# Moving a hybrid encoder block's constants and first transfers ahead of their stages, and a new order of groups in its recurrence

## The chip, the cores and the metric

One core of a Trainium2 chip runs the whole kernel in one launch. The metric is device time in microseconds (us). The engines are TensorE (PE; its weight loads are shown as PEld), VectorE (DVE), ScalarE (ACT), GpSimd (POOL) and SyncE (SP), which issues most of the transfers. A row with a q behind the engine's name (SPq, POOLq) is its sequencer or its DMA queue.

## The reference

The kernel computes one layer of a streaming encoder for 2048 tokens of 1024 features, all in float32. Cut to what matters:

```
u   = rms_norm(x, ln1_g) @ w_in                       # attention and recurrence read columns of u
o_a = diff_attn_mixer(u[:, :1536], ...)               # 4 heads; lam from exp(sum(lq1*lk1)), exp(sum(lq2*lk2))
o_b = rwkv7_mixer(u[:, 1536:], ...)                   # 8 heads of 64:
      # per token: sa = -S kk;  S = S*w + sa b^T + v k^T;  y = S r
h   = x + concat(o_a, o_b) @ w_out
out = h + hier_moe(rms_norm(h, ln2_g), ...)           # 32 experts, 2 of one group of 8 for each token
```

## The kernel before

Five stages follow each other, each a block that all engines enter together once they have ended the one before: `project`, `attend`, `recur`, `merge`, `experts`.

- `project` makes the combined projection by groups of 256 tokens. It keeps the first head's rotated queries and keys in SBUF (`keep["first_head"]`) and writes the rest to scratch in DRAM, among it `chunks`, the recurrence's operands for 32 chunks of 64 tokens, 642 KB each.
- `attend` loads `lams`, `mask` and `ident` (lines 689 to 690), and TensorE and VectorE wait for all three (697, 772). VectorE then works out lambda (775 to 783; ScalarE's exponential for it is line 739) before its first row of maxima (789).
- `recur` runs the recurrence by chunks. Eight heads lie in four pairs, and every small product is 64 wide. Its order is written out by hand. In turn k TensorE works on four chunks at once, named by how far ahead they are: S (chunk k), B (k + 1), A (k + 2), N (k + 3), so 32 chunks take 35 turns. `PE_TURN`, `ACT_TURN` and `DVE_TURN` (823 to 826) give each engine's order in a turn as (group, how far ahead). The engines count their finished groups in one semaphore each, and `on_pe`, `on_act`, `on_dve` turn a group and chunk into the count to wait for. A group is 4 to 16 products into one of four PSUM couples of banks (`ps`), which rotate by one place each turn. TensorE's products have one shared line (937), ScalarE's copies too (1112), and most of VectorE's adds (1147), so they are told apart by their operands.

The groups that matter here, with what their rows show as out<-moving operand,stationary operand:

| Group | What it is | In the rows |
|---|---|---|
| gl, gbk (N) | products inside a chunk; VectorE masks them into `gl` and `g` | rw_ps<-rw_cin |
| bk, v (A) | transposes of b and k, and of v; ScalarE copies them to `rw_tbk` and `rw_sv` | rw_ps<-rw_eye,rw_cin and rw_ps<-rw_ident,rw_cin |
| r1, r2, r3q, r3l, r4 (A), r5 to r8 (B) | steps of inverting a 64x64 triangular matrix, each read back by ScalarE or VectorE before the next | r2 and r3l: rw_w; r3q: rw_q,rw_w; r4: rw_q,rw_l; r6 and r8: rw_ty |
| s0 (B), s1, s2, s3 (S) | solve for sa and add to the state | s1: rw_state,rw_cin; s0: rw_sv,keep_first_head |
| y1, y2 (S) | the output | rw_cin,rw_state and keep_first_head,rw_sv |

r3l is copied by ScalarE to `l8` (`rw_l` in the rows), r4 reads that. s0 of chunk B ends a turn, and s1 adds to its result at the start of the next, waiting first until s0 is complete. The group gl of a turn waits for VectorE's r8 of the turn before. The operands of five chunks are held (`LOADS`); SP loads the next when y1 and the state's update of an old one are done, and `Early.ahead` (1234) issues the merge stage's constants and `w_out` behind the first five.

- `merge` joins both mixers, adds x and routes the tokens, and `experts` runs 64-token blocks of the experts in order. Before its first block VectorE clears `acc` (two buffers), `xf` and `xb`, then makes `te`, from which come the row numbers (`rows`). GpSimd waits for the clearing, writes two columns of zeros to a spare place (1884, it sets the count that the scatters wait for), then gathers the first two blocks' rows (1887).

Of the kernel before, what the change touches and what calls it, by code (L numbers as in the profile page):

```python
# [24 lines left out]
P = 128  # L25
# [10 lines left out]
NPAIR = 4  # L36
# [102 lines left out]
def project(nc, io, dr, first_head):  # L139
    with ExitStack() as ctx:  # L140
        m = Pool(nc, ctx, "pj")
        w_in = m.sb("w_in", [P, KC, N_IN])
# [3 lines left out]
        ident = m.sb("ident", [P, P])  # L146
        ones2 = m.sb("ones2", [P, P])
        cols = m.sb("cols", [P, PC_N])
# [37 lines left out]
        s_aux = m.sem("aux")  # L186
        s_w = [m.sem(f"w{n}") for n in range(4)]
# [51 lines left out]
        def _(sp):  # L239
# [13 lines left out]
            for n in range(2, 4):  # L253
                weights(n)
            for t in range(XT):
                sp.wait_ge(s_tp, t + 1)
                sp.dma_start(xt[:, t, :], io["x"][GT + t * P:GT + (t + 1) * P, :]).then_inc(s_x[t], 16)
# [30 lines left out]
            for t in range(XT):  # L288
                sp.wait_ge(s_x[t], 16 * NG + 32)

# [335 lines left out]
def attend(nc, io, dr, keep):  # L626
    with ExitStack() as ctx:
# [4 lines left out]
        ident = m.sb("ident", [P, P])  # L632
        mask = m.sb("mask", [P, 2, P])
        lams = m.sb("lams", [P, 4, 64])
# [16 lines left out]
        s_const = m.sem("const")  # L651
# [26 lines left out]
        def _(sp):  # L678
# [10 lines left out]
            for dst, src in ((lams[:, :, :], io["lams"]), (mask[:, :, :], io["c_mask"]), (ident[:, :], io["c_ident"])):  # L689
                sp.dma_start(dst, src).then_inc(s_const, 16)  # L690
            load(0)
            for h in range(1, H_A):
                load(h)

        @block.tensor
        def _(pe):
            pe.wait_ge(s_const, 48)
# [73 lines left out]
        def _(dve):  # L771
            dve.wait_ge(s_const, 48)

# [64 lines left out]
def recur(nc, io, dr, keep, ahead):  # L838
    with ExitStack() as ctx:
        m = Pool(nc, ctx, "rw")  # L840
        cin = [m.sb(f"cin{n}", [P, NPAIR, ROW]) for n in range(LOADS)]
        eye = m.sb("eye", [P, C])
        mgbk = m.sb("mgbk", [P, 2, 2 * C])
        mgl = m.sb("mgl", [P, 3, C])
        ident = m.sb("ident", [P, P])
# [3 lines left out]
        tbk = [m.sb(f"tbk{n}", [P, 2, NPAIR, C]) for n in range(RINGS["tbk"])]  # L849
# [13 lines left out]
        s_const = m.sem("const")  # L863
# [12 lines left out]

        def live(c):

            return 0 <= c < NCH
# [8 lines left out]

        def keys(couple):

            return couple.rearrange("p (r a) n -> p r (a n)", r=2)[:, :, 0:NPAIR * C]

        def values(couple, rows):

            return couple[rows, 1::2, 0:2 * C]
# [13 lines left out]
        def _(sp):  # L909
            for dst, src in ((eye[:, :], io["c_eye"]), (mgbk[:, :, :], io["c_mgbk"]), (mgl[:, :, :], io["c_mgl"]),  # L910
                             (ident[:, :], io["c_ident"])):
                sp.dma_start(dst, src).then_inc(s_const, 16)
            for c in range(LOADS):
                sp.dma_start(cin[c][:, :, :], dr["chunks"][c]).then_inc(s_ld[c], 16)
            ahead(sp)
            for c in range(LOADS, NCH):
                sp.wait_ge(s_pe, on_pe["y1", c - LOADS])
                sp.wait_ge(s_dve, on_dve["st", c - LOADS])
                sp.dma_start(cin[c % LOADS][:, :, :], dr["chunks"][c]).then_inc(s_ld[c % LOADS], 16)
# [12 lines left out]
        def _(pe):  # L932
            A, R, V = slice(0, C), slice(C, 2 * C), slice(4 * C, 5 * C)
# [23 lines left out]

            def turn(k):
                S_, B_, A_, N_ = k, k + 1, k + 2, k + 3
                ba, bb, bc, bd = banks(k)  # L960
                xs, xa, xn = cin[S_ % LOADS], cin[A_ % LOADS], cin[N_ % LOADS]
                ga, gn, gs = (g[c % RINGS["g"]] for c in (A_, N_, S_))
                if live(S_):
# [6 lines left out]
                if live(N_):  # L970
                    pe.wait_ge(s_ld[N_ % LOADS], 16 * (N_ // LOADS) + 16)
                    if live(k):
                        pe.wait_ge(s_dve, on_dve["r8", k])
                    for p, r, f, t, u, j in by_features():
                        ins = product(bb[t, j, LO], xn[f, p, A], xn[f, p, b_of(p)])
                    ins.then_inc(s_pe, 1)
                if live(B_):
                    pe.wait_ge(s_dve, on_dve["r4", B_])
                    if live(k - 1):
                        pe.wait_ge(s_act, on_act["y", k - 1])  # L980
                    elif live(k + 1):
                        pe.wait_ge(s_act, on_act["v", k + 1])
                    l = gl[B_ % RINGS["gl"]]
                    for p, r, f, t, u, j in by_features():
                        product(bc[f, p, LO], q2[t, j, :], eye[t, :])
                        ins = product(bc[f, p, HI], l[t, j, 1, :], q2[t, j, :])
                    ins.then_inc(s_pe, 1)
# [1188 lines left out]
```

## Time and profile before

| What | us |
|---|---|
| median of 3 runs | 2983.03 |
| lowest and highest | 2982.71, 2984.04 |
| the profiled execution | 2979.28 |
| its span, first to last instruction | 2977.3 |
| TensorE busy in the span | 2824.1 |
| VectorE, ScalarE, GpSimd busy | 1541.1, 979.8, 644.8 |

Mean granted TensorE clock of the span: 0.981 of full. Rows are those of the profiled execution. Times in a row are the start from the span's begin, then the duration; in square brackets stands how long the engine had been idle and what ended that.

### The profile page before, as it was taken

The page shows a single profiled execution, that of the slowest core. Times are in us where ns is not written, and L with a number is a line of the kernel's source. Part 1 is how long each engine was busy: PE and PEld are TensorE (multiplying, and loading weights), DVE is VectorE, ACT ScalarE, POOL GpSimd, SP SyncE. Part 2 cuts the span into 40 slices and gives each one's busy share as a digit, 9 for nine tenths or more (in the row PEclk, how much of TensorE's full clock was granted, in tenths as well). Part 3 has the DMA queues.
Part 4 walks back from the last instruction along what each step waited for, and adds up shares of the span by engine and source line. Part 5 has one row for each costly group of instructions (what it writes and reads, how often), then busy time and mean ns, then how long its engine had stood idle before and what let it go on. Part 6 is the DMA issues. An engine that isn't in the chain of part 4 may idle for free. (4 is left out here: it accounts for less than half of the span.)

```text
span 2977.3 us, 61430 instructions
## 1 busy us (share of the span) xinstructions
PE 2824.1 (95%) x23130; PEld 1777.5 (60%) x23131; DVE 1541.1 (52%) x3560; ACT 979.8 (33%) x2303; POOL 644.8 (22%) x812
## 2 busy tenths in 40 slices
PE   8999999999979999989999799994999999999999
PEld 6787878778756666679998555452333333333333
DVE  4677676777768988834444577763111111111111
ACT  3343344334437777734444333331000000000000
POOL 0000000000015555611111001002333333333333
PEclk9999999999989999999999999996999999999999
DMA  7111121121130110041111132253889788787663
GB/s 253 61 64 60 48 79 56 50 72 60 52 116 1 44 44 1 1 169 60 62 57 57 45 113 91 94 183 94 286 301 339 249 299 314 276 292 246 251 218 124
DMA packets 187586, 393.03 MB, mean 132 GB/s; under 512 B 15866, under 2 KB 74106, under 8 KB 186576
## 3 DMA queue, kind: packets, MB, share of 16 engines
q1 hardware_dynamic: 166848, 339.34, 33.0%
q0 software_dynamic: 20512, 50.54, 4.9%
q8 instruction: 159, 2.61, 0.4%
q14 instruction: 67, 0.55, 0.1%
HBM read 325.22 MB, written 78.22 MB: 136 GB/s over the span
## 5 line engine op out<-in xcount | busy, mean ns | idle before, releaser
L328 PE MATMUL pj_big<-pj_xnT,pj_w_in 128*128 128x256 f32 x2816 | 634.6, 381 | 2.1 <-DVE pj_xnT L467 1.5
L328 PEld LDWEIGHTS pj_big<-pj_xnT,pj_w_in 128*128 128x128 f32 x2816 | 537.0, 191 | 83.2 <-issue 5.7
L1921 PE MATMUL ex_pgu<-keep_res,ex_xT 128*64 128x512 f32 x2560 | 568.5, 597 | 0.0
L1921 PEld LDWEIGHTS ex_pgu<-keep_res,ex_xT 128*64 128x64 f32 x2560 | 177.1, 137 | 334.5 <-issue 334.5
L2029 DVE TENSOR_TENSOR ex_hh<-ex_sg,ex_pgu 128x256 f32<-128x256 f32 x80 | 33.7, 421 | 583.5 <-ACT ex_sg L1994 583.5
L1939 PE MATMUL ex_py<-keep_res,ex_hT 128*64 128x512 f32 x1280 | 288.3, 592 | 1.0 <-DVE ex_yb L2037 1.0
L767 POOL TENSOR_SCALAR at_tt<-at_e,at_cf 128x512 f32<-128x512 f32 (+3 forms) x160 | 219.7, 1376 | 176.7 <-DVE at_pd L811 164.1
L1440 PE MATMUL mg_po<-keep_res,mg_mix 128*128 128x512 f32 x512 | 232.5, 611 | 6.9 <-DVE mg_mix L1743 6.9
L298 POOL TENSOR_TENSOR pj_m<-pj_qn,pj_cosin 128x256 f32<-128x256 f32 x64 | 46.6, 729 | 823.4 <-DVE pj_qn L528 597.0
L1994 ACT ACTIVATE ex_sg<-ex_pgu 128x256 f32<-128x256 f32 x80 | 30.7, 384 | 581.4 <-PE ex_pgu L1921 581.4
L746 ACT ACTIVATE at_e<-at_sc,at_nmx 128x512 f32<-128x512 f32 (+3 forms) x320 | 197.0, 623 | 61.6 <-DVE at_nmx L789 59.3
L1939 PEld LDWEIGHTS ex_py<-keep_res,ex_hT 128*64 128x64 f32 x1280 | 91.9, 137 | 183.3 <-issue 182.1
L789 DVE TENSOR_REDUCE at_nmx<-at_sc 128x2 f32<-128x1024 f32 (+3 forms) x160 | 169.5, 1060 | 26.5 <-PE at_sc L708 17.8
L1440 PEld LDWEIGHTS mg_po<-keep_res,mg_mix 128*128 128x128 f32 x512 | 98.3, 196 | 124.1 <-issue 116.3
L1851 POOL DMA_INDIRECT ex_xb<-hn_s,ex_idx x80 | 82.5, 1031 | 361.4 <-PE ex_px L1914 351.0
L2037 DVE SCALAR_TENSOR_TENSOR ex_yb<-ex_py,ex_gates,ex_acc 128x512 f32<-128x512 f32 x80 | 60.1, 751 | 181.1 <-PE ex_py L1939 181.1
L732 PE MATMUL at_op<-at_vh,at_pt 128*128 128x128 f32 x1088 | 148.2, 276 | 0.8 <-ACT at_pt L758 0.8
L732 PEld LDWEIGHTS at_op<-at_vh,at_pt 128*128 128x128 f32 x1088 | 135.1, 193 | 1.4 <-ACT at_pt L758 1.0
L526 DVE RECIPROCAL pj_qrr<-pj_qrr 128x256 f32<-128x256 f32 x64 | 111.9, 1749 | 21.6 <-ACT pj_qrr L441 21.6
L1998 ACT ACTIVATE ex_hT<-ex_phT 128x256 f32<-128x256 f32 x80 | 30.7, 384 | 270.2 <-PE ex_phT L1929 270.2
L927 POOL TENSOR_TENSOR rw_w<-keep_first_head,rw_eye 64x256 f32<-64x256 f32 x64 | 46.1, 720 | 337.7 <-DVE keep_first_head L1158 335.8
L328 PE MATMUL pj_big<-pj_w_in,pj_xnT 128*128 128x512 f32 x256 | 112.5, 592 | 0.0
(288 smaller groups left out, 4370.7 us busy)
## 6 DMA issues: line engine op xcount, KB each, us to landing
keep_res<-in_w_exp_gate SPq DMA_DIRECT2D x32, 2048.0 KB, 8.9
keep_res<-in_w_exp_up SPq DMA_DIRECT2D x32, 2048.0 KB, 16.0
keep_res<-in_w_exp_down SPq DMA_DIRECT2D x32, 2048.0 KB, 8.7
chunks_s<-pj_st SPq DMA_DIRECT2D x32, 642.0 KB, 3.9
rw_cin<-chunks_s SPq DMA_DIRECT2D x32, 642.0 KB, 4.1
pj_xt<-in_x SPq DMA_DIRECT2D x20, 512.0 KB, 3.8
mg_xin<-in_x SPq DMA_DIRECT2D x8, 1024.0 KB, 7.3
out<-mg_hb SPq DMA_DIRECT2D x16, 512.0 KB, 3.4
```

The source lines that it names most:

```text
L298: pool.tensor_tensor(m1[:, p % 2, :], qn[:, p % 2, :], cosin[:, 0, :], ALU.mult).then_inc(s_m1, 1)
L328: ins = pe.matmul(out, lhs, rhs, start=(k == 0), stop=(k == KC - 1))
L526: link(dve, ch, dve.reciprocal(qrr[:, p % 2, :], qrr[:, p % 2, :]))
L732: ins = pe.matmul(op[t % 2][:, 0:P], pt[:, u % 2, b * P:(b + 1) * P], vh[h % 2][:, n, :], start=(n == 0), stop=(n == i))
L746: ins = act.activation(e[:, u % RE, c, 0:w], sc[u % 2][:, c, 0:w], ACT.Exp, bias=nmx[:, t % RE, c, s:s + 1], accum_out=sums[:, t % RE, c, ...
L767: pool.tensor_scalar(tt[:, u % 2, 0:w], e[:, u % RE, 1, 0:w], cf[:, t % RE, 1, s:s + 1], None, ALU.mult).then_inc(s_t, 1)
L789: dve.tensor_reduce(nmx[:, t % RE, :, s], sc[u % 2][:, :, 0:w], AX, ALU.max, negate=True)\
L1440: ins = pe.matmul(po[:, n, :], mix[:, x, k, tok], w_out[:, k, 512 * n:512 * n + 512], start=(k == 0), stop=(k == KC - 1))
L1851: pool.indirect_dma_start(xb[:, :], None, hn2, bass.IndirectOffsetOnAxis(idx[:, 0:1], 0), bounds_check=LAST, oob_is_err=False).then_inc(s_ ...
L1921: ins = pe.matmul(pgu[j * BT:(j + 1) * BT, :, :], lhs, wgu[x][:, k, :, j * HE:(j + 1) * HE], start=(k == 0), stop=(k == KC - 1))
L1939: ins = pe.matmul(py[n * BT:(n + 1) * BT, :], hT[:, part, j * BT:(j + 1) * BT], wd[x][:, 2 * j + part, n * HD:(n + 1) * HD], start=(part = ...
L2037: dve.scalar_tensor_tensor(yb[x][:, :], py[:, :], gates[:, bass.ds(b, 1)], acc[x][:, :], ALU.mult, ALU.add).then_inc(s_yb, 1)
```

## The change

Five things change:

1. `ident` and `cols` are loaded once, in `project`, and kept. `mask` and `lams` are loaded in `project` behind its weights (`lams` in the space of `tb`, which is used later). `attend` waits for no constant.
2. The recurrence's constants and chunk 0 (in the space of `w_out`) are loaded in `attend`, behind the second head's loads. `recur` loads chunks 1 to 5 first, and `w_out` once chunk 0 is used up.
3. In a turn of the recurrence bk and v become one group, bkv: twelve products of 128 rows against the 128x128 identity. ScalarE copies it in three copies that count as one group.
4. The order within a turn is new on three engines. s0 belongs to the same turn as s1.
5. In `experts` GpSimd clears `xf` and `xb` itself, gathers the first two blocks before it writes the spare place (now one row of 64 numbers, taken from `rec`), and VectorE clears `acc` after the row numbers.

```diff
-PE_TURN = (("s1", 0), ("gl", 3), ("r5", 1), ("gbk", 3), ("bk", 2), ("r1", 2), ("s2", 0), ("r2", 2), ("s3", 0), ("v", 2), ("r6", 1),
-           ("r3q", 2), ("r3l", 2), ("r7", 1), ("y1", 0), ("r4", 2), ("y2", 0), ("r8", 1), ("s0", 1))
-ACT_TURN = (("s1", 0), ("r5", 1), ("bk", 2), ("r1", 2), ("sa", 0), ("r2", 2), ("v", 2), ("r3l", 2), ("r7", 1), ("y", 0))
-DVE_TURN = (("gl", 3), ("gbk", 3), ("sa", 0), ("r2", 2), ("s3", 0), ("r6", 1), ("st", 0), ("r3q", 2), ("r4", 2), ("r8", 1))
+PE_TURN = (("gl", 3), ("gbk", 3), ("s0", 0), ("r5", 1), ("s1", 0), ("bkv", 2), ("r1", 2), ("s2", 0), ("r2", 2), ("r6", 1), ("y1", 0),
+           ("s3", 0), ("y2", 0), ("r7", 1), ("r3q", 2), ("r3l", 2), ("r8", 1), ("r4", 2))
+ACT_TURN = (("r5", 1), ("s1", 0), ("r1", 2), ("sa", 0), ("bkv", 2), ("r2", 2), ("r7", 1), ("r3l", 2), ("y", 0))
+DVE_TURN = (("gl", 3), ("gbk", 3), ("sa", 0), ("r2", 2), ("r6", 1), ("s3", 0), ("st", 0), ("r3q", 2), ("r8", 1), ("r4", 2))
...
-            for dst, src in ((lams[:, :, :], io["lams"]), (mask[:, :, :], io["c_mask"]), (ident[:, :], io["c_ident"])):
-                sp.dma_start(dst, src).then_inc(s_const, 16)
             load(0)
             for h in range(1, H_A):
                 load(h)
+                if h == 1:
+                    for dst, src in ((seam["eye"][:, :], io["c_eye"]), (seam["mgbk"][:, :, :], io["c_mgbk"]),
+                                     (seam["mgl"][:, :, :], io["c_mgl"]), (seam["cin"][:, :, :], dr["chunks"][0])):
+                        sp.dma_start(dst, src).then_inc(seam["s_ready"], 16)
...
+                if live(S_):
+                    for p, r, f, t, u, j in by_tokens():
+                        ins = product(ba[t, j, LO], gs[u, r, p, LO], sv[S_ % RINGS["sv"]][u, p, features(r)], first(p), False)
+                    ins.then_inc(s_pe, 1)
...
-                    for p, r, f, t, u, j in by_features():
-                        ins = product(keys(bb)[:, r, p * C:(p + 1) * C], xa[f, p, BK], eye[f, :])
+                    for q in range(2):
+                        for column, swap, to in ((b_of, 0, PAIR), (k_of, 1, PAIR), (v_of, 1, PAIR2)):
+                            for h in range(2):
+                                p = q + 2 * h
+                                ins = product(bb[HALVES[h ^ swap], p, to], xa[:, p, column(p)], ident[:, :])
...
                 if live(B_):
+                    pe.wait_ge(s_act, on_act["r7", B_])
+                    if live(A_):
+                        pe.wait_ge(s_act, on_act["r3l", A_])
+                    elif live(S_):
+                        pe.wait_ge(s_dve, on_dve["s3", S_])
                     for p, r, f, t, u, j in by_features():
+                        ins = product(ba[t, j, LO], ty[1][f, p, LO], ty[1][f, p, HI])
...
+                    copy("bkv", A_, (v[low, 0:2, :], bb[low, 0:2, PAIR2]), (v[top, 2:4, :], bb[top, 2:4, PAIR2]),
+                         (tbk[A_ % RINGS["tbk"]][:, :, :], bb[:, :, PAIR]))
...
+            pool.memset(xf[:, :], 0.0)
+            pool.memset(xb[:, :], 0.0).then_inc(s_clear, 1)
             pool.wait_ge(s_clear, 1)
-            for n in range(2):
-                pool.dma_start(dr["spare"][n], acc[0][:, 0:1]).then_inc(o_y, 16)
             pool.wait_ge(s_rows, 1)
             for b, (to, sem) in enumerate(((xf, s_xf), (xb, s_x))):
                 pool.indirect_dma_start(to[:, :], None, hn2, bass.IndirectOffsetOnAxis(rows[:, b:b + 1], 0),
                                         bounds_check=LAST, oob_is_err=False).then_inc(sem, 16)
+            pool.wait_ge(s_cleared, 1)
+            for n in range(2):
+                pool.dma_start(dr["spare"][n, 0:4 * NT].rearrange("p o -> o p"),
+                               keep["rec"][0:1].rearrange("p t n w -> p (t n w)")).then_inc(o_y, 16)
```

## Rows read from the trace of the kernel before

**Rows 1.** The page: busy time by engine, and one of its costliest groups.

```profile
PE 2824.1 (95%) x23130; PEld 1777.5 (60%) x23131; DVE 1541.1 (52%) x3560; ACT 979.8 (33%) x2303; POOL 644.8 (22%) x812
...
L767 POOL TENSOR_SCALAR at_tt<-at_e,at_cf 128x512 f32<-128x512 f32 (+3 forms) x160 | 219.7, 1376 | 176.7 <-DVE at_pd L811 164.1
```

**Rows 2.** Busy time by stretch: stretch, its length, then each engine, clock, DMA.

```profile
1277.00:1681.00 404.00, 381.99 (x11520) 354.23 (x11520) 174.91 (x352) 165.44 (x352) 46.09 (x64) 0.99 0.22 72
...
1275.00:1281.00 6.00, 3.88 (x54) 3.44 (x56) 2.07 (x3) 0.00 (x0) 0.00 (x0) 0.50 1.01 405
```

**Rows 3.** Timeline at the border between `project` and `attend`.

```profile
871.58 1.28 ACT L739 ACT_TABLE_LOAD   x1 [5.72 <-PEq L140]
...
876.19 0.80 PE L708 MATMUL at_sc<-keep_first_head 64*128 64x128 f32 x4 [10.98 <-DMA at_ident<-in_c_ident]
...
877.51 0.43 DVE L789 TENSOR_REDUCE at_nmx<-at_sc 128x2 f32<-128x256 f32 x1
```

**Rows 4.** Timeline at the border between `attend` and `recur`.

```profile
1270.98 0.33 SPq L912 DMA_DIRECT2D rw_eye<-in_c_eye  x1
...
1272.77 2.69 SPq L914 DMA_DIRECT2D rw_cin<-chunks_s  x5
...
1277.12 4.87 PE L937 MATMUL rw_ps<-rw_cin 64*64 64x64 f32 x64 [6.77 <-DMA rw_cin<-chunks_s]
...
1279.76 2.04 PEld L937 LDWEIGHTS rw_ps<-rw_cin 64*64 64x64 f32 x32 [0.22 <-issue]
```

**Rows 5.** Timeline at the start of `experts`.

```profile
2048.72 1.02 DVE L2041 MEMSET ex_acc<- 128x512 f32 x2 [9.41 <-PEq L1264]
...
2051.14 1.18 POOL L1884 DMA_DIRECT2D spare_s<-ex_acc  x2 [7.10 <-DVE ex_xb L2043]
...
2052.64 1.08 POOL L1887 DMA_INDIRECT ex_xf<-hn_s,ex_rows  x1 [0.32 <-DVE ex_rows L2052]
...
2063.67 1.12 PE L1914 MATMUL ex_px<-keep_ident,ex_xf 128*128 128x128 f32 x4 [11.52 <-DMA ex_xf<-hn_s,ex_rows]
```

**Rows 6.** Timeline of weight loads in one turn: s1, bk, r2, v, r3q, r3l, r8, s1.

```profile
1450.84 0.35 PEld L937 LDWEIGHTS rw_ps<-rw_state,rw_cin 64*64 64x64 f32 x16 [0.27 <-DVE rw_q L1147]
...
1452.95 0.98 PEld L937 LDWEIGHTS rw_ps<-rw_eye,rw_cin 64*128 64x128 f32 x16
...
1455.84 1.42 PEld L937 LDWEIGHTS rw_ps<-rw_w 64*64 64x64 f32 x32 [0.37 <-ACT rw_w L1112]
...
1457.79 0.42 PEld L937 LDWEIGHTS rw_ps<-rw_ident,rw_cin 128*64 128x64 f32 x8
...
1458.62 0.57 PEld L937 LDWEIGHTS rw_ps<-rw_q,rw_w 64*64 64x64 f32 x16
1459.08 0.58 PEld L937 LDWEIGHTS rw_ps<-rw_w 64*64 64x64 f32 x16
...
1461.83 0.32 PEld L937 LDWEIGHTS rw_ps<-rw_ty 64*64 64x64 f32 x16
...
1462.88 0.35 PEld L937 LDWEIGHTS rw_ps<-rw_state,rw_cin 64*64 64x64 f32 x16 [0.27 <-DVE rw_q L1147]
```

**Rows 7.** Timelines of ScalarE and VectorE in that turn: bk, sa, v, r8.

```profile
1454.12 0.60 ACT L1112 ACTIVATE rw_tbk<-rw_ps 128x512 f32<-128x512 f32 x1 [1.34 <-PE rw_ps L937]
...
1455.69 0.36 ACT L1112 ACTIVATE rw_sv<-rw_ps 64x256 f32<-64x256 f32 x1
...
1458.53 0.77 ACT L1112 ACTIVATE rw_sv<-rw_ps 64x256 f32<-64x256 f32 x2
...
1462.42 0.42 DVE L1147 TENSOR_TENSOR rw_q<-rw_ps,rw_q 128x256 f32<-128x256 f32 x1 [0.61 <-PE rw_ps L937]
```

**Rows 8.** Transfers from 2038 to 2070: KB each, median us to landing.

```profile
spare_s<-ex_acc POOLq DMA_DIRECT2D x2, 0.5 KB, 7.9
...
ex_xb<-hn_s,ex_idx POOLq DMA_INDIRECT x1, 3.3
```

**Rows 9.** Timeline of weight loads in the recurrence's second turn: r4 behind r3l.

```profile
1289.46 0.54 PEld L937 LDWEIGHTS rw_ps<-rw_q,rw_l 64*64 64x64 f32 x15 [0.67 <-DVE rw_q L1147]
```

More of the change, by code:

```diff
@@ L186, in project @@
         s_aux = m.sem("aux")
+        s_later = m.sem("later")
         s_w = [m.sem(f"w{n}") for n in range(4)]
@@ L254, in _ @@
                 weights(n)
+            for dst, src in ((keep["lams"][:, :, :], io["lams"]), (keep["mask"][:, :, :], io["c_mask"])):
+                sp.dma_start(dst, src).then_inc(s_later, 16)
             for t in range(XT):
@@ L631, in attend @@
         vh = [m.sb(f"vh{x}", [P, NT, P]) for x in range(2)]
-        ident = m.sb("ident", [P, P])
-        mask = m.sb("mask", [P, 2, P])
-        lams = m.sb("lams", [P, 4, 64])
+        ident, mask, lams = keep["ident"], keep["mask"], keep["lams"]
         lam = m.sb("lam", [P, 8])
@@ L875, in recur, with chunk @@
         W0, PAIR2 = slice(2 * C, 3 * C), slice(2 * C, 4 * C)
+        def chunk(c):
+            return seam["cin"] if c == 0 else cin[(c - 1) % LOADS]
         def live(c):
@@ L909, in _ @@
         def _(sp):
[L910 to L916, printed above, removed]
+            for c in range(1, 1 + LOADS):
+                sp.dma_start(chunk(c)[:, :, :], dr["chunks"][c]).then_inc(s_ld[(c - 1) % LOADS], 16)
+            early.ahead(sp)
+            sp.wait_ge(s_pe, on_pe["y1", 0])
+            sp.wait_ge(s_dve, on_dve["st", 0])
+            early.load_w_out(sp)
+            for c in range(1 + LOADS, NCH):
                 sp.wait_ge(s_pe, on_pe["y1", c - LOADS])
                 sp.wait_ge(s_dve, on_dve["st", c - LOADS])
-                sp.dma_start(cin[c % LOADS][:, :, :], dr["chunks"][c]).then_inc(s_ld[c % LOADS], 16)
+                sp.dma_start(chunk(c)[:, :, :], dr["chunks"][c]).then_inc(s_ld[(c - 1) % LOADS], 16)
         @block.gpsimd
@@ L1033, in turn @@
                     ins.then_inc(s_pe, 1)
-                if live(S_):
+                if live(B_):
+                    pe.wait_ge(s_act, on_act["r5", B_])
+                    for p, r, f, t, u, j in by_features():
+                        ins = product(bc[t, j, LO], ty[0][f, p, LO], ty[0][f, p, HI])
+                    ins.then_inc(s_pe, 1)
+                if live(S_):
+                    if live(A_):
+                        pe.wait_ge(s_act, on_act["bkv", A_])
+                    for p, r, f, t, u, j in by_features():
+                        ins = product(bb[f, p, LO], state[S_ % 2][f, p, :], xs[f, p, R], first(p), False)
+                    ins.then_inc(s_pe, 1)
                     pe.wait_ge(s_act, on_act["sa", S_])
@@ L1181, in turn @@
                     add("r3q", A_, q1, bd[:, :, LO], q0)
-                    dve.wait_ge(s_dve, on_dve["r3q", A_])
-                    add("r4", A_, q2, bd[:, :, LO], q1)
                 if live(B_):
@@ L2038, in add @@
                                          ALU.mult, ALU.add).then_inc(s_yb, 1)
-            for buf in acc:
-                dve.memset(buf[:, :], 0.0)
-            dve.memset(xf[:, :], 0.0)
-            dve.memset(xb[:, :], 0.0).then_inc(s_clear, 1)
             dve.sem_inc(s_yb, 1)
@@ L2052, in _ @@
                 dve.tensor_copy(rows[:, n * P:(n + 1) * P], ptab[:, n, 0, 0:P]).then_inc(s_rows, 1)
+            for buf in acc:
+                ins = dve.memset(buf[:, :], 0.0)
+            ins.then_inc(s_cleared, 1)
             dve.wait_ge(s_gates, 2)
```

173 lines of the change are left out of this document (73 added, 100 removed).

## The prediction

> **What bounds the kernel now.** I read the page's busy shares first. TensorE is busy in 95% of the span [rows 1], and no other engine comes near. So time is won or lost where TensorE waits. I then read the busy time by stretch for the recurrence: 404 us, TensorE busy 382.0, granted clock 0.99 [rows 2]. It too is bound by its one instruction stream, and both parts of the change can be read as "which TensorE wait goes, which comes". Next came the timeline at the three borders of stages that the change touches. Before attention TensorE idles 10.98 us, last for a constant's transfer [rows 3]. Before the recurrence it idles 6.77 us for the first chunk [rows 4]. Before the experts it starts at 2063.67, 11.0 us after its first gather was issued [rows 5]. Last I read one turn of the recurrence from the weight loads, since these show the order and spacing of the groups [rows 6], with some of the copies and adds beside it [rows 7]. A turn is 12.04 us (s1 starts at 1450.84 and 1462.88). A group of eight 64x64 products on two quarters of the array shows 0.57 us of loads, but the next group starts 0.46 after it (1458.62 and 1459.08). So the true loss of a wait is its idle time on the loads plus 0.09 to 0.11 of lost overlap.
>
> The sum is made against the profiled execution (span 2977.3 us, time 2979.3); the median shown is 2983.0, so I add the sum of differences to 2983.0.
>
> **Border before attention.** lams, mask and ident no longer load here; two of them are queued behind the projection's weights, at the very start, at two SP issues of some 0.4 us (one constant's issue is 0.33 [rows 4]), and SP is not what TensorE waits for there. All engines may start at 871.58, where ScalarE does. The new limit is not TensorE but lambda: VectorE's product and sum end near 872.2, ScalarE's table load ends at 871.58 + 1.28 = 872.86, its exponential and VectorE's two small operations take some 0.6 more. VectorE's first maximum then starts near 873.5 in place of 877.51 [rows 3]. **Gain 4.0 us.** Bounds: 2, if the array's half clock after the idle time (as in the 0.50 of the next border [rows 2]) lasts longer into the tiles, and 6, if the shorter idle time spares part of it.
>
> **Border before the recurrence.** Constants and chunk 0 are there already. SP's first issue is at 1270.98, so gl and gbk of chunk 0 start near 1271.4, behind one memset, not at 1277.12 [rows 4]. But the next gl needs chunk 1, now SP's first issue at 1270.98. Chunk 0 took 4.33 us from its issue at 1272.77 to the first product, behind four small transfers. So chunk 1 is there near 1275.2, and gl of chunk 1 starts then in place of 1279.76: 4.5 us. What is late next is thus the same transfer, one chunk on. The half clock of this stretch (0.50 from 1275 to 1281 [rows 2]) need not appear with two short idles in place of a long one: up to 0.8 us on the two groups that remain. **Gain 5.3 us**, bounds 4 and 7. The w_out transfer moves behind chunk 0's last use, some 30 us later; it has until the merge stage, near 1691, and later chunk loads have more than a turn (12 us) of slack for a 4 us landing, so I cost that at nothing. The cover is that turn: without it each late load would cost its own landing.
>
> **Border before the experts.** VectorE's four memsets of 128x512 leave its queue ahead of the row numbers, which come 2 x 1.02 = 2.0 us earlier [rows 5]. The two gather buffers are cleared by GpSimd now. No row shows such a GpSimd memset. Below it is VectorE's, 1.02 us for two of this size; above, GpSimd's scaling of the same 128x512, 1376 ns each or 2.75 for two [rows 1]. It has one input less, so I take 2.0 for both. From 2048.6 they end near 2050.6, level with the row numbers (2052.64 - 2.0). Then the gathers go first, and the two `spare` writes, which stood ahead of them in GpSimd's queue (1.18 us of issue [rows 5], 7.9 to land [rows 8]), go behind. A gather of the same kind and size a few microseconds later landed in 3.3 us [rows 8]; the first one took 11.0 with the `spare` writes ahead of it. Issue at 2050.9, landing after 4.2 (between these, near the short one, since only the second gather runs beside it): 2055.1. **Gain 8.5 us**, bounds 2 (only the earlier issue counts) and 10. The acc memsets and `spare` now lie beside the gathers; their cover is these 4 us.
>
> The old `spare` writes are 128 pieces of 4 bytes each, the new ones one row of 256 bytes each. The Trainium skill ("DMA: Bandwidth & Descriptors", Specifications) says that a transfer below 512 B is done as a read, a change and a write. The 7.9 us landing of 0.5 KB agrees for the old form, and no row shows the new one. By that rule the 11.0 us landing is the `spare` writes' doing and this border gives its 8.5; without it the third rival below holds, with a gain of 2.
>
> **The transposes in one group.** bk's loads (8 products) run 0.98 us and v's (4) 0.42 [rows 6]; less the overlap that is 0.87 for bk, and for v, whose last product is twice as wide, near 0.40: 1.27 together. bkv has 12 products shaped like v's: 12 x 0.10 = 1.2, or 12 x 0.13 = 1.6 if v's slot hides some of the array's switch behind it. I take 1.26, since a longer run has no more switches; so no change in TensorE's work; bounds -0.1 and +0.3 us a turn. ScalarE copies as much as before: 0.60 for bk and 0.77 for v's two [rows 7].
>
> **The new order, in waits.** Old waits:
> - r2 waits for ScalarE's copy of r1, with s2 alone between: idle 0.37, so 0.46 lost [rows 6]. The new order has r1, s2, r2 again: this stays.
> - s1 waits until s0 is through the array: idle 0.27, so 0.36 lost. Now r5 stands between them: gone.
>
> New waits:
> - r8 comes right behind r3l and must wait until ScalarE has copied r3l out of the bank that r8 writes. Before, r7 and y1 filled that time. The recurrence's first turns, where nothing fills it, show the bare wait: 0.67 idle after r3l's loads [rows 9]. With the lost overlap 0.76; I take 0.75, bounds 0.6 and 0.85.
> - gl, now first of the next turn, needs VectorE's r8. From r8's first load at 1461.83 to the end of that add at 1462.42 + 0.42 = 1462.84 [rows 7], and 0.04 on, is 1.05; r8's own slot, half of a two-quarter group's (0.23), and r4's (0.46 to 0.53) fill 0.72: 0.33 lost. Before, s0 and s1 stood there.
> - y1 writes the bank that ScalarE's bkv copies empty. These start behind the copy of sa, at 1455.69 + 0.36 = 1456.05 in the old turn's count and take 1.37: 1457.42, and 0.05 for the wait to end. TensorE reaches y1 after r2 (1455.84 and 1.34) and r6 (0.24), at 1457.42. I take 0.07, bounds 0 and 0.3.
>
> Sum of a turn: 0.75 + 0.33 + 0.07 - 0.36 = **0.79 us longer**, so 12.8 us. Queued behind the waiting r8 are r4, then gl and gbk, and behind these the whole next turn; nothing lies beside it. r3l meets r8 in 31 of the 35 turns, r8 meets gl in 29. That makes 30 x 0.79 = 23.7 us; the short turns at either end have less of all, some 0.8 us. **Loss 23 us**, bounds 17 (0.6 a turn) and 30 (1.0).
>
> The switch of the array between 64x64, 64x128 and 128x64 products costs some 0.2 us where the rows show one (v starts at 1457.79 and fills 0.40, r3q starts at 1458.62, and between them lies r6 with 0.23). There are six switches a turn in the old order and six in the new, so it cancels. The Trainium skill ("TensorEngine Tiling (Array Packing)", Key Properties) states that changing the tiling mode drains the engine, and a reader who saw "all transposes in one group" might expect a switch fewer from it. Counted by that rule too the number stays six, and the gain of one drain, 0.2 us a turn or 6 us in all, isn't there.
>
> **Sum.** 23 - 4.0 - 5.3 - 8.5 = +5 us: 2988 us. Its own range, from the bounds above, 2978 to 2998.
>
> **Rivals.**
> - *The order costs little or gains.* Place: r8 behind r3l. If the wait for the copy were 0.2 in place of 0.75, for instance because ScalarE's r7 and r3l copies and r4 overlap better than the startup row shows, a turn would be no longer than before, and the borders' 18 us remain: 2965 us. It decides from a turn below 0.6 us longer, where 30 turns eat less than the 18. For it: r3l's slot fell beside r7 before and the sum of small terms may hide cover. Against: the bare wait stands in a row.
> - *The turn grows by 1.0 to 1.1.* bkv at 1.5, ScalarE's copy late, y1 waiting 0.3: 30 x 1.05 = 31, less 18: 2996 us. For it: ScalarE now has 1.37 us in one piece ahead of r2's copy. Against: r3q needs that only 2.5 us later.
> - *The expert gathers gain only the earlier issue.* The first gather of a stage might land late by itself, not for the `spare` writes: gain 2, so 2994 us. For it: every engine had been idle there. Against: the 3.5 us gather a few microseconds later.
>
> **Numbers.** A measurement of this kernel tells from no change about 0.2%, 6 us. My forecast 0.52, of which 0.28 lies within 6 us, 0.21 above and 0.03 below. Order costs little 0.18, all faster. Turn grows by 1.05: 0.17, slower but for 0.01. Gathers gain little 0.09, 0.06 of it slower. Something else 0.04, evenly. Faster 0.22, within 0.34, slower 0.44. The range is 2974 to 3000: it takes in the bounds of my sum and both slower rivals, and leaves most of the faster one out.
>
> **What would show it.** In the profile after: a turn of 12.8 us; an idle time of 0.6 to 0.8 us ahead of r8 put down to ScalarE's copy `rw_l`, and one near 0.3 ahead of gl put down to VectorE; none between s0 and s1. TensorE's first attention group near 871.6 and VectorE's first maximum near 873.5; a wait for the second chunk that ends near 1275 by the old count; first transposes of the experts 4 to 5 us after their gather. Wrong it would be if ScalarE's copies ran in other gaps than I drew, or if the turn is bound by something that the old order hid.

## The result, and the profile after

The changed kernel takes 2989.7 us (median of 14 runs, 2986.2 to 2993.9) beside 2983.1 us of the kernel before (2980.0 to 2986.3): a ratio of 1.0025, with a 95% interval of 1.0017 to 1.0032. Measured a second time, beside the experiments, it was 1.0029 (1.0019 to 1.0040). It is slower by some 7 to 9 us; 2988 was forecast. The three borders did shrink and the recurrence did grow, so what is seen is a difference of two larger numbers.

First the page and the busy time of the recurrence (start and end of the stretch, its length, then busy time and count for TensorE, its weight loads, VectorE, ScalarE and GpSimd, then granted clock, DMA share and GB/s):

```profile
span 2987.5 us, 61365 instructions
PE 2828.1 (95%) x23130; PEld 1775.8 (59%) x23131; DVE 1543.1 (52%) x3558; ACT 971.2 (33%) x2303; POOL 645.4 (22%) x814
```

```profile
1268.00:1699.00 431.00, 384.79 (x11504) 352.99 (x11504) 177.52 (x352) 155.39 (x352) 46.26 (x64) 1.00 0.20 68
1267.00:1273.00 6.00, 3.62 (x62) 3.28 (x64) 3.48 (x5) 0.00 (x0) 1.44 (x2) 0.84 0.83 302
1272.00:1274.00 2.00, 2.00 (x22) 1.78 (x20) 0.95 (x2) 0.00 (x0) 0.00 (x0) 0.50 1.03 424
```

TensorE's work in the recurrence is nearly what it was (384.8 us here, 382.0 in [rows 2]), but the stretch from its first group to the merge stage has gone from 404 to 431.7 us. Of the 27 us between the two stretches shown 24 are idle time of TensorE.

The timelines of the changed kernel at the three borders, to be held against [rows 3], [rows 4] and [rows 5]:

```profile
872.62 1.28 ACT L740 ACT_TABLE_LOAD   x1 [5.72 <-PEq L140]
872.65 0.80 PE L709 MATMUL at_sc<-keep_first_head 64*128 64x128 f32 x4 [6.40 <-PEq L140]
...
874.53 0.42 DVE L788 TENSOR_REDUCE at_nmx<-at_sc 128x2 f32<-128x256 f32 x1
```

```profile
1267.50 1.55 PE L928 MATMUL rw_ps<-keep_res 64*64 64x64 f32 x32 [1.15 <-DVE rw_state L1182]
1270.93 2.37 PE L928 MATMUL rw_ps<-rw_cin 64*64 64x64 f32 x30 [1.87 <-DMA rw_cin<-chunks_s]
```

```profile
2068.03 0.53 POOL L1877 MEMSET ex_xf<- 128x512 f32 x1 [4.56 <-POOLq L1259]
2068.50 0.64 POOL L1878 MEMSET ex_xb<- 128x512 f32 x1
2070.36 1.02 POOL L1882 DMA_INDIRECT ex_xf<-hn_s,ex_rows  x1 [1.22 <-DVE ex_rows L2047]
...
2072.68 1.11 POOL L1886 DMA_DIRECT2D spare_s<-keep_rec  x2
```

```profile
2073.70 1.11 PE L1913 MATMUL ex_px<-keep_ident,ex_xf 128*128 128x128 f32 x4 [3.77 <-DMA ex_xf<-hn_s,ex_rows]
```

TensorE's idle time at the start of attention no longer ends with a transfer. VectorE's first maximum comes 1.91 us behind the stage's start, not 5.93. The recurrence starts on chunk 0 behind a memset of the state, and what is late next is chunk 1: 1.87 us of idle time, put down to its DMA. In the experts' stage the first gather lands 3.3 us behind its issue, so TensorE's first transposes come 5.65 us behind the stage's start (2068.05) in place of 15.10 (2063.67 less 2048.57). In the other eleven profiles with the changed borders VectorE's maximum comes at 1.91 or 1.92 us too, and in the nine of them with the new start of `experts` the transposes at 5.7 to 5.9.

One turn of the recurrence, weight loads as in [rows 6], then the waits of the weight loads from 1400 to 1640 (total us, times, longest):

```profile
1452.66 0.35 PEld L928 LDWEIGHTS rw_ps<-rw_ty 64*64 64x64 f32 x16 [0.67 <-ACT rw_l L1105]
1452.88 0.59 PEld L928 LDWEIGHTS rw_ps<-rw_q,rw_l 64*64 64x64 f32 x16
1453.82 1.39 PEld L928 LDWEIGHTS rw_ps<-rw_cin 64*64 64x64 f32 x32 [0.34 <-issue]
...
1456.75 1.29 PEld L928 LDWEIGHTS rw_ps<-keep_ident,rw_cin 128*64 128x64 f32 x24
...
1460.06 1.41 PEld L928 LDWEIGHTS rw_ps<-rw_w 64*64 64x64 f32 x31 [0.37 <-ACT rw_w L1105]
...
1461.62 0.55 PEld L928 LDWEIGHTS rw_ps<-rw_cin,rw_state 64*64 64x64 f32 x16
...
1465.55 0.35 PEld L928 LDWEIGHTS rw_ps<-rw_ty 64*64 64x64 f32 x16 [0.67 <-ACT rw_l L1105]
```

```profile
PEld rw_ps L928 <- ACT rw_l L1105: 12.8, 19, 0.7
PEld rw_ps L928 <- issue: 10.3, 39, 0.7
PEld rw_ps L928 <- ACT rw_w L1105: 6.6, 18, 0.4
```

From r8 (1452.66) to r8 (1465.55) a turn is 12.89 us; it was 12.03 to 12.04. Ahead of r8 stands the forecast wait for ScalarE's copy of r3l, 0.67 us in each of 19 turns. Ahead of gl (1453.82) stand 0.34 us. The row of the loads calls them "issue"; the products' own row at that place names VectorE (`[0.23 <-DVE rw_q L1141]`). y1 (1461.62) waits for nothing.

In the two profiled executions the stages divide the difference so (us, after less before): projections +1.0; attention from its start to the recurrence's first product -10.7 (405.5 to 394.9); the recurrence +27.7 (404.0 to 431.7); merge +1.4; start of the experts' stage -9.45; the rest +0.2. The sum is 10.2 where the medians differ by 6.6, because the profiled execution of the kernel before lay 3.8 us below its own median.

A stage's time moves by itself from one profile to the next, so not every term is an effect. The merge stage, the same work in all fourteen profiles of this document, took 367.1 to 371.7 us. Attention up to the recurrence's first product took 405.5 us in both profiles with the old borders and 395.9 to 396.2 in the other eleven with the new ones: 9.3 to 9.6 is what that border and the next gained, and the 10.7 above holds 1 us of chance.

### The profile page after: what moved, and what is told of

Its sections match the earlier page's. It is cut to its first block and busy times, and to the rows that moved or that the text cites. A ratio compares the mean times of both kernels' runs of the same rounds, so it can differ in the third digit from the quotient of the medians.

```text
span 2987.5 us, 61365 instructions
## 1 busy us (share of the span) xinstructions
PE 2828.1 (95%) x23130; PEld 1775.8 (59%) x23131; DVE 1543.1 (52%) x3558; ACT 971.2 (33%) x2303; POOL 645.4 (22%) x814
## 5 line engine op out<-in xcount | busy, mean ns | idle before, releaser
L918 POOL TENSOR_TENSOR rw_w<-keep_first_head,seam_eye 64x256 f32<-64x256 f32 x64 | 46.3, 723 | 358.0 <-DVE keep_first_head L1152 356.2
L810 DVE SCALAR_TENSOR_TENSOR at_pd<-at_e,at_cf,at_tt 128x512 f32<-128x512 f32 (+3 forms) x160 | 110.0, 688 | 4.7 <-POOL at_tt L768 2.4
```

What stands on the lines that cost most here:

```text
L810: dve.scalar_tensor_tensor(pd[:, u % 4, 0:w], e[:, u % RE, 0, 0:w], cf[:, t % RE, 0, s:s + 1], tt[:, u % 2, 0:w], ALU.mult, ALU.add)\
```

## The experiments

Beside each time stands the ratio to the kernel before from runs on the same chip, since the kernel before itself moved by 0.1% between them. "Turn" is the distance between two of ScalarE's copies of s1 in the steady part.

**Order alone, borders alone.** The change cut in two: the kernel before with the new group order and joined transposes, and the changed kernel with the turn of before.

```
-PE_TURN = (("s1", 0), ("gl", 3), ("r5", 1), ("gbk", 3), ("bk", 2), ("r1", 2), ...
+PE_TURN = (("gl", 3), ("gbk", 3), ("s0", 0), ("r5", 1), ("s1", 0), ("bkv", 2), ...
 (first kernel: on the kernel before; second kernel: the reverse, on the changed one)
```

> The recurrence's new order and joined transposes alone, with the three borders as they were before. Theory (the order costs, the borders pay): the turn goes from 12.00 to 12.9 us, as in the changed kernel's trace, so 30 turns cost some 27 us and the time is 3010 us (3006 to 3013); the first gl of the recurrence stays some 6.8 us behind the stage's start and the experts' first transpose 15 us behind theirs. Rival (the new order costs little by itself, the turn is long only beside the loads and copies that the borders moved): turn within 0.3 us of 12.00, time below 2993 us.

> The three changed borders with the recurrence's turn, its transposes in two groups and its order as before. Theory: attention gains 5, the recurrence's start 4.8, the experts' start 9.4, less 2.4 that the stages of projections and merge grew in the changed kernel's trace: 17 us off, 2966 us (2962 to 2971), with a turn of 12.00 us. Rival (the borders' gains are given back by transfers that now collide): 2975 us or above, with a turn or a stage that grows by 8 us or more.

Measured: the order alone 1.0074 (1.0057 to 1.0091), +22 us, turn 12.89. The borders alone 0.9958 (0.9944 to 0.9972), -12.5 us, turn 12.03. Together they make +9.5 us, which the changed kernel's 1.0025 and 1.0029 (7.5 to 8.6 us) bear out. So the first theory held in kind and both rivals fell. But the order cost 22, not 27, and the borders gave 12.5, not 17. For the borders the trace of the second kernel has a part of it. Its waits of the weight loads from 1400 to 1640:

```profile
PEld rw_ps L936 <- ACT rw_w L1112: 7.3, 20, 0.4
PEld rw_ps L936 <- DVE rw_q L1147: 5.1, 19, 0.3
PEld rw_ps L936 <- issue: 4.2, 22, 0.6
```

These are the steady turns of before, unchanged. Yet the stretch from the first product to the merge stage takes 407.0 us and not 404.0. The starts of ScalarE's copies show where: the second turn has 14.77 us where the kernel before has 12.66, and the filling turns ahead of the first copy have 29.4 in place of 27.8. This became a question of its own (below, w_out).

**Joined transposes in the old order.** The changed borders, the joined group at v's old place, ScalarE's copy behind that of r2.

```
+PE_TURN = s0 s1 gl r5 gbk r1 s2 r2 s3 bkv r6 r3q r3l r7 y1 r4 y2 r8
+ACT_TURN = s1 r5 r1 sa r2 bkv r3l r7 y
```

> The borders changed, the order of before, and only the transposes joined: one group at the place where v's transposes stood (behind s3), ScalarE's joined copy behind r2's. Theory (joining is neutral): b and k's 0.98 us and v's 0.42 go, 1.29 to 1.46 come, turn 12.07 us (11.8 to 12.3), 2 us more than the kernel with the borders alone (6 less to 9 more). Rival (the joined group makes the turn long, its 1.37 us copy on ScalarE holding the small copies back): turn 12.4 to 12.9 us, 12 to 27 us more than with the borders alone.

Measured: 0.9938 (0.9920 to 0.9956), turn 11.97 us. The steady turn is 0.06 us shorter than with two groups, so joining is neutral or a little better, and the rival fell: the long turn isn't the joined group's doing. Against the borders alone the time is 6 us less, at the edge of what was expected. In the traces the turns are 3 us less in sum, and the first, filling turns 4 us less (first product to first copy of s1: 25.2 us in place of 29.4). Of these 4 us 1.6 are one stop of TensorE at 1289.66 in the borders' trace, of the kind told below under w_out, which isn't in this one. The order of the waits that stand there changed too, and the rest was not separated.

**The wait of r8 behind r3l, covered in two ways.** First r3l ahead of r3q:

```
-           ("s3", 0), ("y2", 0), ("r7", 1), ("r3q", 2), ("r3l", 2), ("r8", 1), ("r4", 2))
+           ("s3", 0), ("y2", 0), ("r7", 1), ("r3l", 2), ("r3q", 2), ("r8", 1), ("r4", 2))
```

> The changed kernel with one thing turned round: r3l stands ahead of r3q on TensorE, so that r3q's 0.46 us covers a part of the wait of r8 for ScalarE's copy of r3l (0.67 us in the changed kernel's trace). Theory (that wait is a term of the turn): the wait falls to some 0.3 us, with up to 0.2 us of a new wait of r4 for VectorE's r3q; turn 12.55 us in place of 12.89, 10 us less over 30 turns, 2980 us (2976 to 2984). Rival (the turn is set by a chain through ScalarE or VectorE, and the wait only shows its slack): the wait goes and comes back in front of another group, turn within 0.1 us of 12.89, time within 2 us of 2990.

Measured: 0.9990 (0.9980 to 1.0000), some 10 us less than the changed kernel; turn 12.48 us. Its waits from 1400 to 1640:

```profile
PEld rw_ps L928 <- issue: 8.2, 41, 1.0
PEld rw_ps L928 <- ACT rw_w L1105: 7.0, 19, 0.4
PEld rw_ps L928 <- ACT rw_l L1105: 5.1, 19, 0.3
```

The wait fell from 12.8 us in 19 turns to 5.1 and nothing took its place. The rival (a chain through the other engines sets the turn) fell. Second, y2 moved into the gap:

```
-           ("s3", 0), ("y2", 0), ("r7", 1), ("r3q", 2), ("r3l", 2), ("r8", 1), ("r4", 2))
+           ("s3", 0), ("r7", 1), ("r3q", 2), ("r3l", 2), ("y2", 0), ("r8", 1), ("r4", 2))
```

> The changed kernel with y2 moved from its place behind s3 to between r3l and r8, so that r8 no longer follows directly on r3l. y2 and s3 use the array in the same way and now stand apart, which adds two changes of array mode. Theory (a turn is the sum of the groups, their waits and 0.2 us for each change of mode): the wait of 0.67 to 0.72 us goes, 0.4 us comes, turn 12.57 us in place of 12.89, 10 us less over 30 turns: ratio 0.9995 of the time before where the changed kernel has 1.0025 to 1.0029. Rival (changes of mode cost nothing of their own): turn 12.2 us, 21 us less, ratio 0.996.

Measured: 0.9986 (0.9976 to 0.9996), turn 12.43 us, between the two expectations and nearer to the first. The weight loads of r3l, y2 and r8 in its timeline:

```profile
1446.95 0.57 PEld L928 LDWEIGHTS rw_ps<-rw_w 64*64 64x64 f32 x15
1447.59 0.55 PEld L928 LDWEIGHTS rw_ps<-keep_first_head,rw_sv 128*64 128x64 f32 x16
1448.20 0.34 PEld L928 LDWEIGHTS rw_ps<-rw_ty 64*64 64x64 f32 x16
```

From y2 (128-row products) to r8 it is 0.61 us. This alone doesn't price the change of array mode, since ScalarE's copy of r3l ends at 1448.07 there and may still be what lets r8 start. The changed kernel has the change without such a wait, at s3, y2 and r7:

```profile
1449.35 0.55 PEld L928 LDWEIGHTS rw_ps<-rw_sv,rw_tbk 128*64 128x64 f32 x16
1449.81 0.55 PEld L928 LDWEIGHTS rw_ps<-keep_first_head,rw_sv 128*64 128x64 f32 x16
1450.43 0.23 PEld L928 LDWEIGHTS rw_ps<-seam_eye,rw_q 64*64 64x64 f32 x8
```

Two groups of one mode follow each other after 0.46 us (s3, y2), and r7 of the other mode after 0.62. A change of array mode thus costs 0.16 us, not 0.2. In the changed kernel r8 starts 1.24 us after r3l, of which 0.78 is not r3l's own slot. That gap has room for y2's 0.46 and two changes of 0.16, and the turn loses just the 0.46 that y2 took before.

**w_out.** In the changed kernel's second turn (16.35 us) TensorE stops in the middle of a group. The transposes' weight loads, and the issue of w_out 6 us before:

```profile
1304.91 0.37 SPq L1235 DMA_DIRECT2D keep_res<-in_w_out  x1
```

```profile
1310.61 0.96 PEld L928 LDWEIGHTS rw_ps<-keep_ident,rw_cin 128*64 128x64 f32 x17
...
1313.51 0.41 PEld L928 LDWEIGHTS rw_ps<-keep_ident,rw_cin 128*64 128x64 f32 x7 [1.94 <-issue]
```

No semaphore is named, and the 4 MB of w_out kept the DMA engines busy meanwhile (14.3 us from issue to landing). The DMA view shows that it was the instructions that came late: they have a queue of their own, on which they come in packets of 16 KB. From 1304.3 to 1311.1 it lists w_out's queue alone, and from 1311.1 to 1312.2 one packet of instructions beside it:

```profile
q1 hardware_dynamic: 434, 1.78, 72.2%
```

```profile
q8 instruction: 1, 0.02, 5.5%
```

That packet landed at 1312.14, and TensorE went on at 1313.51. The next one landed at 1318.23, and the next stop (1.18 us) ended at 1319.62. The same holds in all fourteen traces. Behind its first 8 us the recurrence has 29 waits of 0.94 us or more of its weight loads with "issue" for a releaser, and each ended 1.2 to 1.6 us after a packet of this queue had landed. The changed kernel's second profile has a stop of 2.21 us at the same product, and after it the half clock (0.50 from 1319 to 1321). The kernel before has two such stops in its filling turns, where its own w_out, issued at 1284.72, and other loads moved:

```profile
1295.40 0.19 PEld L937 LDWEIGHTS rw_ps<-keep_first_head,rw_gl 64*64 64x64 f32 x4 [1.25 <-issue]
1302.14 0.13 PEld L937 LDWEIGHTS rw_ps<-rw_q,rw_gl 64*64 64x64 f32 x1 [1.24 <-issue]
```

The changed kernel was then given w_out in eight parts, one behind each chunk's load:

```
-            early.load_w_out(sp)                      # behind y1 and st of chunk 0
 ...
+                if c - 1 - LOADS < KC:
+                    early.load_w_out(sp, c - 1 - LOADS)
```

> The changed kernel with the 4 MB load of w_out cut into eight of 512 KB, one behind each chunk's load, where the changed kernel issues it whole behind turn 0. There the trace shows TensorE's instructions themselves coming late, 1.94 and 1.18 us in the middle of two groups, and a second turn of 16.35 us where the others have 12.9. Theory (the one long transfer holds back what feeds TensorE its instructions): the second turn falls to 13.5 us or less and the time by 3 us, to some 2987 us. Rival (the gaps come wherever the 4 MB are moved, in sum the same): the second turn is shorter, others longer, the time within 1 us of the changed kernel's 2989.7.

> The changed kernel itself again, beside the three that follow, so that they are read against it on one chip: 1.0025 of the time before (1.0017 to 1.0032). Both theories on w_out's load expect the same of it.

> The kernel of e5_w_out_parts with more rounds. Its trace had no long second turn (12.88 us in place of 16.35), its time did not show the 3 us. Theory (the gap in the second turn belongs to every execution): 3 us less than c_changed_again. Rival (the gaps from late instructions fall in other places in each execution and have the same sum): within 1 us of c_changed_again.

The same 14 us, first in the changed kernel, then with w_out in parts (columns as above):

```profile
1305.00:1319.00 14.00, 10.88 (x306) 9.65 (x300) 4.70 (x9) 4.83 (x11) 1.44 (x2) 1.00 0.79 302
```

```profile
1305.00:1319.00 14.00, 12.63 (x385) 11.58 (x380) 5.97 (x12) 5.64 (x14) 1.45 (x2) 1.00 0.04 8
```

With the DMA engines at 0.79 TensorE gets 306 products done, with them at 0.04 it gets 385. The second turn falls to 12.88 us, and to 13.09 in the second profile, in place of 16.35 and 16.41. The instruction packet that started at 1311.16 starts at 1308.82 here. In the traces the theory held for this turn. The time didn't show it: 1.0029 (1.0019 to 1.0038) and 1.0027 (1.0016 to 1.0039) beside 1.0025 and 1.0029 for w_out whole. These intervals are as wide as the 3 us in question. Other turns of the second kernel have 0.7 to 1.1 us more (13.6 to 14.0 us, at three places in each profile; the changed kernel has two such turns in its first profile). From first to last copy of s1 its two profiles take 393.8 us, and four profiles with w_out whole (those of the changed kernel and of the two on `spare` below) 395.1 to 397.3. So some of the loss moves to other turns, as the rival says, and 1.3 to 3.5 us are gained in the traces. What of it the other executions have stays open.

It doesn't take 4 MB: the joined transposes in the old order have stops of 0.91 us at 1455.11 and 1.16 at 1600.66, where nothing but one chunk of 642 KB was loaded in the 8 us before. Both stops ended 1.4 to 1.5 us after a packet of instructions had landed.

**The writes to `spare`.** The changed kernel with these two writes ahead of the first gathers again, once in their form of before, once in the new one:

```
+            for n in range(2):            # first kernel: 128 partitions, one element each
+                pool.dma_start(dr["spare"][n], keep["rec"][:, 0, 0, 0:1]).then_inc(o_y, 16)
+            # second kernel: the new form, one partition's 64 elements, at the same place
             pool.wait_ge(s_rows, 1)
             for b, (to, sem) in enumerate(((xf, s_xf), (xb, s_x))):
```

> The changed kernel with the two writes to spare in their form of before (128 pieces of 4 bytes each) and ahead of the first two gathers again, but from a buffer that is ready, so that they wait for nothing. Theory (the small writes hold up the gathers that are queued behind them): the gather of xf is issued 1.5 us later and lands 11 us behind its issue in place of 3.3, so that TensorE's first transposes come 14 to 15 us behind the stage's start in place of 5.65. Rival (the gathers gained their earlier issue alone, the slow landing belonged to the loads that ran beside them): 7 to 8 us behind the stage's start.

> The changed kernel with its two writes to spare in their present form (one row of 64 floats, written to 64 rows of 4 bytes) but ahead of the first two gathers. In the old form, 128 pieces of 4 bytes, ahead of them, the first transposes came 13.2 us behind the stage's start, against 5.65. Theory (it is the count of 4-byte pieces at the target that the gathers queue behind): half the pieces, half of the delay: 9 to 10.5 us. Rival (it is the order alone, any two writes ahead cost the same): 13 us; second rival (pieces from one row go as one): 7 to 7.5 us, the two issues alone.

TensorE's first transposes in the two, old form first; the stages start at 2068.62 and 2069.07:

```profile
2081.83 1.11 PE L1911 MATMUL ex_px<-keep_ident,ex_xf 128*128 128x128 f32 x4 [11.33 <-DMA ex_xf<-hn_s,ex_rows]
```

```profile
2076.15 1.11 PE L1912 MATMUL ex_px<-keep_ident,ex_xf 128*128 128x128 f32 x4 [5.19 <-DMA ex_xf<-hn_s,ex_rows]
```

With the old form ahead of the gathers the transposes come 13.2 us behind the stage's start, where the changed kernel has 5.65; with the new form ahead they come after 7.1: the gather is issued 0.5 us later than in the changed kernel and lands 4.3 us after its issue in place of 3.3. So of the 9.45 us that this border gained, the order alone (new form behind rather than ahead) is 1.4, and the old form's delay of the gathers is 6.1 (13.2 less 7.1). The other 1.9 lies between the kernel before and the one with the old form ahead: 1.2 of earlier issue (2.9 us behind the stage's start in place of 4.1) and 0.7 of landing, and of such size is what chance does here too, since the profile of the order alone, with this border as before, has 14.15 us in place of 15.10. Both kernels have one execution each, 2997.3 and 2991.7 us, 7.5 and 1.9 above the changed kernel's profiled one. The first theory was nearly right for the old form (14 to 15 us expected), and for the new one the second rival was: the forms differ in kind, not by half. The DMA view, old form first, once up to the first packet of the gathers (from 2071 to 2073.2, and from 2071.5 to 2073.5) and once behind it (to 2084 and 2079):

```profile
q0 software_dynamic: 64, 0.00, 2.2%
q0 software_dynamic: 160, 0.48, 61.3%
```

```profile
q0 software_dynamic: 64, 0.00, 1.5%
q0 software_dynamic: 160, 0.48, 38.3%
```

The packets are as many in both forms. The trace records a write to `spare` as 16 packets, of 32 bytes in the old form and 16 in the new, so it says nothing of single pieces. These small packets take next to no time themselves: 0.022 x 2.2 us x 16 engines = 0.8 us in all in the old form. What takes long is the 4 KB packets of the gathers behind them: 0.613 x 10.8 x 16 = 106 us of DMA time in the old form, 0.383 x 5.5 x 16 = 34 us in the new, and single ones up to 7.2 and 1.6 us. So the old form holds up the gathers' own packets; how it does so no row shows. The Trainium skill ("DMA: Bandwidth & Descriptors", Specifications) puts both forms below its 512 B bound, so that rule doesn't tell them apart. They differ in their source (128 partitions or one), and which property is the costly one was not tried.

**A better order.** The same sums were used to look for an order in which no group but r2 comes soon behind the one whose copy it needs:

```
+PE_TURN = s0 r5 gbk s1 r1 gl s2 r2 s3 bkv r6 r3q r3l r7 y1 r4 y2 r8
+ACT_TURN = r5 s1 r1 sa r2 bkv r3l r7 y
+DVE_TURN = gbk sa gl r2 s3 r6 st r3q r4 r8
```

> The changed borders and the joined transposes with another order: s0 r5 gbk s1 r1 gl s2 r2 s3 bkv r6 r3q r3l r7 y1 r4 y2 r8, the copies and adds in the order that follows from it. No group follows directly on the one whose copy it waits for, but r2 (behind r1's copy, 0.2 us), and y2 and bkv cost four changes of array mode in place of six. Theory (the waits found in the traces and the groups' own times add up to the turn): 11.5 us a turn, 1.4 less than the changed kernel, 42 us less over 30 turns: 2948 us (2943 to 2955). Rival (a wait not in the sum, or weight loads, hold the turn near the 11.97 us of the joined old order): 2961 us or more.

> The kernel of b1_new_order with w_out in eight parts and with the second chunk too loaded during attention. Theory: 1.9 us less than b1_new_order (2947.7) for the chunk, and for w_out 3 us less or nothing, as e5_again shows: 2943 to 2946. Rival: the first turns are held by VectorE and ScalarE, and none of it comes: 2948.

Measured: the new order 2947.7 us, 0.9884 (0.9867 to 0.9901), 35 us faster than the kernel before and 42 faster than the changed one, as summed. The waits did this: by the loads' shapes there are six changes of array mode in a turn here as in the changed kernel, and none is saved, against what was expected. Its turn is 11.46 us, and these are all the waits of its weight loads from 1400 to 1640 that the view lists:

```profile
PEld rw_ps L927 <- issue: 6.2, 25, 1.0
PEld rw_ps L927 <- ACT rw_ty L1140: 0.6, 1, 0.6
PEld rw_ps L927 <- ACT rw_w L1140: 0.4, 1, 0.4
```

Even the wait for r1's copy, which both kernels had in every turn, stands there only once; r2 still starts 0.68 us after s2 (1426.28 and 1426.96), so 0.2 of it is left, as expected. The second kernel (two chunks ahead, w_out in parts) was no faster: 0.9889 (0.9873 to 0.9904). The first products of chunk 1 no longer wait for a transfer; in its timeline they run in one row with those of chunk 0:

```profile
1269.72 2.48 PEld L927 LDWEIGHTS rw_ps<-keep_res 64*128 64x128 f32 x48 [1.32 <-issue]
```

The first copy of s1 came 1.3 us sooner behind it, but turns of 13.24, 12.70 and 12.29 us stood in the trace where the others have 11.46. In them stand stops of 1.82, 1.34 and 0.76 us that end 1.3 to 1.6 us after an instruction packet landed; in the 9 us ahead of the first a chunk and a part of w_out were loaded back to back. Its mean turn was 11.51 us, that of b1_new_order 11.41. Of the 5 us expected nothing can be measured. The time is what the rival said, though not for its reason: the chunk's 1.3 us did come, and late instructions took them back.

## Why the prediction was right

The time was forecast at 2988 and came at 2989.7, within the range, and the ratio of 1.0025 lies just above the bound of 0.2%. The mechanism was the forecast one: three borders shrink, and the turn grows by r8's and gl's new waits. That the sum came so near is in part luck, since terms of 1 to 3 us were off and partly cancelled. By its own steps:

- *Border before attention, -4.0 (2 to 6):* -4.0 as VectorE's maximum shows it, from the stage's own start (5.93 to 1.91). With the 5.6 of the next border at chunk 0 this is the 9.6 that attention up to the recurrence's first product shrank by in most profiles. Whether the moved loads were free is open: in the two profiles of kernels without them attention starts at 871.6 and 872.7, in the twelve with them at 872.4 to 874.4, and these ranges overlap.
- *Border before the recurrence, -5.3 (4 to 7):* right in mechanism (chunk 1 is late next, 1.87 us), 4.8 in size at gl of chunk 1, counted from the end of attention. Without its term for the clock the step says 4.5. That term, up to 0.8 for a half clock that need not appear, was wrong: chunk 0's group ran at full clock (its 32 loads in 1.39 us), but behind the wait for chunk 1 the granted clock was 0.50 (1272 to 1274), and that chunk's 32 loads took 2.29 us, where [rows 4] has 2.04.
- *w_out at nothing:* here a step failed. It was costed by when the data are due. In the trace its transfer held back TensorE's instructions for some 3 us in the second turn (16.35 us in place of 12.9). Nothing in the sum stood for that. The kernel before had paid something like it already, 2.5 us in its filling turns, where the changed kernel has one stop of 1.20; so the three stops of the changed kernel are 1.8 us more than the two before. How much of this the time holds was not resolved.
- *Border before the experts, -8.5 (2 to 10):* -9.45. GpSimd's two memsets took 1.1 us and not the 2.0 taken from rows of other work; the landing took 3.3, not 4.2. The writes to `spare` were the cause, as the forms compared show.
- *Joined transposes, 0 (-0.1 to +0.3 a turn):* -0.06 a turn in the old order. bkv's slot is 1.46 us with a change of mode in it, where 1.26 was taken without one.
- *The turn, +0.79 (0.6 to 1.0):* +0.86. r8's wait 0.67 idle and 0.11 of overlap, 0.78 for 0.75. gl 0.34 idle and as much overlap, 0.45 for the 0.33 lost that was forecast: this is the term most off. y1 none for 0.07, s1's 0.36 gone as forecast. 0.78 + 0.45 - 0.36 is 0.87. 30 turns at 0.79 gave 23; the order alone measured 22, and 24 from product to merge stage in its trace.
- *The sum:* 23 less 17.8 gave +5. Measured alone, the parts are +22 and -12.5, and the changed kernel is 6.6 to 8.6 us above the kernel before. So the forecast missed most on the side of the borders, 12.5 for 17.8. Stops for late instructions are a part of that. The rest is spread over stages that move by themselves: in the profile of the borders alone attention starts 2.1 us later and the merge stage takes 0.5 more than before.

The rival "the order costs little" fell by the order alone and by the 0.67 us in each turn. "The turn grows by 1.05" was 0.2 a turn too much. "The gathers gain only the earlier issue" was refuted by the old form put back.

## What to carry over

Where one instruction stream is 95% busy and unrolled, write out for each group of a turn the engine that last reads the bank it writes. Then give the group a place at least one copy (here 0.8 us) behind that bank's last writer: the sums of groups, waits and mode changes foretold the turns of 12.89, 12.48, 12.43 and 11.46 us to within 0.15 us. Loading the first operands of a stage ahead is worth the idle time at its border. But look at what is queued in front of the load that is late next, and price a transfer of megabytes by what shares the DMA engines with it too, and not only by when its data are due: in unrolled code that is also the engines' own instructions.

## What the runs showed of the hardware that was not expected

- TensorE can stop in the middle of a group for want of instructions while one 4 MB load runs: 1.94 and 1.18 us in one turn at a DMA share of 0.79, with no semaphore involved; with 512 KB parts the same turn had none of it. Stops of some 1 us stand behind single loads of 642 KB too.
- Instructions come as packets of 16 KB on a DMA queue of their own, and TensorE went on 1.2 to 1.6 us after the late one had landed.
- Two writes of 128 x 4 bytes from 128 partitions delay a gather queued behind them by 6 us more than two of 64 x 4 bytes from one partition do; the time is in the gathers' own packets, not in those of the writes.
- A change between 64x64 and 128x64 products costs TensorE 0.16 us.
- GpSimd clears 128x512 floats in 0.53 to 0.64 us.
